# Two transformer blocks on one core: layer-norm factors from per-token sums, the later half's sums moved into the next stage, layers written out, the second block's first units in halves

## The reference, cut to what matters

```
y = _group_rmsnorm(mix, mix_g[l]) @ w_o[l]
x = _layernorm(ALPHA * x + y, ln1_g[l], ln1_b[l])
f = (jax.nn.silu(x @ w_gate[l]) * (x @ w_up[l])) @ w_down[l]
x = _layernorm(ALPHA * x + f, ln2_g[l], ln2_b[l])
...
h = x + 0.5 * swiglu(rms_norm(x, ffn1_norm[l]), ffn1_gate[l], ffn1_up[l], ffn1_down[l])
```

## Time and profile before

| | |
|---|---|
| median of 3 runs | 3297.21 us |
| the profiled execution's own time | 3301.32 us |
| its span, first to last instruction | 3299.5 us |
| TensorE matmuls busy | 3186.5 us, 97% of the span |
| VectorE, ScalarE, GpSimd busy | 1520.4, 714.4, 1967.7 us |
| granted TensorE clock, mean | 0.982 |

### The profile page before, as it was taken

One profiled execution on the slowest core, in us unless ns is written; L12 is line 12 of the kernel. 1 busy time (PEld: TensorE's weight loads), 2 busy tenths in 40 slices (PEclk: granted clock), 3 DMA queues, 4 the chain that ended last, 5 costly groups with the idle time before them and its releaser, 6 DMA issues.

```text
span 3299.5 us, 44938 instructions
## 1 busy us (share of the span) xinstructions
PE 3186.5 (97%) x15410; PEld 2620.2 (79%) x15410; DVE 1520.4 (46%) x1976; ACT 714.4 (22%) x1450; POOL 1967.7 (60%) x1566
## 2 busy tenths in 40 slices
PE   8998999989989999699999999999999999999998
PEld 7777888877778888588887778888888887778886
DVE  6577332275773231644327574432344237664422
ACT  3353110034532110411102231110111112321110
POOL 6334766653346666377766556776677666277763
PEclk9999999999999999899999999999999999999999
DMA  4111322221112222122223212222222232122231
GB/s 170 52 39 52 108 95 96 96 91 58 39 52 90 95 95 96 52 95 96 100 97 105 78 65 94 97 96 96 97 95 95 96 112 96 39 96 95 95 99 61
DMA packets 82023, 286.47 MB, mean 87 GB/s; under 512 B 9531, under 2 KB 13020, under 8 KB 81628
## 3 DMA queue, kind: packets, MB, share of 16 engines
q1 hardware_dynamic: 76032, 275.81, 24.8%
q10 hardware_dynamic: 5852, 8.78, 0.8%
HBM read 280.89 MB, written 3.67 MB: 86 GB/s over the span
## 4 chain that ended last, share of the span: by engine, by line
PE 91%; DVE 5%; issue 2%; ACT 1%; POOL 1%; DMA 0%; DVEq 0%; SPq 0%; ACTq 0%; POOLq 0%
PE bank_v L462 19%; PE bank_v L464 19%; PE bank_v L463 19%; PE bank_a L462 8%; PE bank_a L464 8%; PE bank_a L463 8%; PE bank_v L677 1%; PE bank_a L656 1%; PE bank_s L810 1%; PE bank_s L695 1%; PE bank_v L825 1%; PE bank_a L501 0%; DVE lru_x L1954 0%; PE bank_s L813 0%; PE bank_s L685 0%
## 5 line engine op out<-in xcount | busy, mean ns | idle before, releaser
L436 POOL TENSOR_TENSOR w_lo<-raw,w_hi 128x1024 fp32r<-128x1024 f32 x520 | 1319.4, 2537 | 41.7
L433 POOL TENSOR_TENSOR zero<-zero 128x1 f32<-128x1 f32 x520 | 128.0, 246 | 1253.8 <-PE bank_v L464 900.4
L462 PE MATMUL bank_v<-xn_hi,w_hi 128*128 128x512 f32 (+1 forms) x1680 | 645.5, 384 | 8.9 <-DVE resid L1505 4.5
L464 PE MATMUL bank_v<-xn_hi,w_lo 128*128 128x512 f32 (+1 forms) x1680 | 637.0, 379 | 0.0
L463 PE MATMUL bank_v<-xn_lo,w_hi 128*128 128x512 f32 (+1 forms) x1680 | 636.9, 379 | 0.0
L434 POOL CAST w_hi<-raw 128x1024 fp32r<-128x1024 f32 x520 | 555.0, 1067 | 0.0
L462 PE MATMUL bank_a<-xn_hi,w_hi 128*128 128x512 f32 (+1 forms) x1232 | 473.9, 385 | 40.3 <-DVE xn_lo L1477 21.5
L463 PE MATMUL bank_a<-xn_lo,w_hi 128*128 128x512 f32 (+1 forms) x1232 | 468.7, 380 | 0.0
L464 PE MATMUL bank_a<-xn_hi,w_lo 128*128 128x512 f32 (+1 forms) x1232 | 468.6, 380 | 0.0
L462 PE MATMUL bank_v<-h_hi,w_hi 128*128 128x512 f32 (+1 forms) x1100 | 419.7, 382 | 0.0
L464 PE MATMUL bank_v<-h_hi,w_lo 128*128 128x512 f32 (+1 forms) x1100 | 418.6, 381 | 0.0
(11 more groups left out here) (341 smaller groups left out, 3359.8 us busy)
## 6 DMA issues: line engine op xcount, KB each, us to landing
raw<-in_w_stream SPq DMA_DIRECT2D x520, 512.0 KB, 3.2
rope<-in_rope ACTq DMA_DIRECT2D x2, 1024.0 KB, 4.9
da_v<-t_rows ACTq DMA_DIRECT2D x2, 1024.0 KB, 5.7
out<-resid SPq DMA_DIRECT2D x4, 512.0 KB, 2.6
t_rows<-t_row ACTq DMA_DIRECT2D x1, 1536.0 KB, 5.7
resid<-in_x SPq DMA_DIRECT2D x4, 256.0 KB, 3.7
resid<-in_x ACTq DMA_DIRECT2D x4, 256.0 KB, 8.8
mla_v<-in_alibi ACTq DMA_DIRECT2D x2, 512.0 KB, 5.9
```

Of the source, the lines that this page charges most:

```text
L433: pool.tensor_tensor(zero[:, 1:2], zero[:, 0:1], zero[:, 0:1], ALU.add)
L436: pool.tensor_tensor(w_lo[:, u, :], raw[:, u, :], w_hi[:, u, :].bitcast(F32), ALU.subtract).then_inc(*w_split.done(("unit", u)))
L462: pe.matmul(out, lhs_hi, rhs_hi, start=first, stop=False)
L464: return pe.matmul(out, lhs_lo, rhs_hi, start=False, stop=last)
```

## The change

1. `ln_stats` makes sums per token instead of rows: the sums are now the stationary operand and one column of ones the moving one. Eight fp32 matmuls of 128 x 1 (two tiles, two sums, two sources) put mean and square sums of a half into four columns of `bank_s[0]`.
2. `factors(s)` works on tiles of 128 x 2. It then multiplies the identity by the reciprocal and by the offset, two 128 x 128 tiles each, and `ln_spread(tag, s)` on TensorE multiplies ones by these diagonals (two fp32 matmuls with 256 columns). `apply` reads both factors from two banks of PSUM instead of from `work` in SBUF.
3. `ln_stats(0)` moves to step 5 of the first, `ln_spread(0)` to step 5 of the second chunk of s=1 in `project_out`; in `down` they stand after steps 5 and 17 of the last chunk's s=1.
4. `ln_stats(1)` and `ln_spread(1)` of both norms stand in the next stage's `project_halves`, after its steps 1 and 8 of s=0. VectorE does factors(1) inside apply(0), after its step 5, ScalarE after its chunk 4. The lag is 3 instead of 4.
5. A root of one value stands at the head of each norm on ScalarE.
6. The last ln2 writes `xn_hi` and `xn_lo` with the second block's gain in its own passes; `gained("first")` goes. The first four units of the second block (gate0, up0, k=0,1) run in `project_halves` (`ffn_halves`). ScalarE makes the squares for `rms1` after apply(1), and then copies gate0's banks out; VectorE adds the squares, then copies up0's banks out; the sums for `rms1` and their spreading stand behind gate1,0 and up1,0.
7. The two layers of each block are written out instead of looped, with constants as semaphore targets (`laps`, `within`, `find` in `Counts` and `Signal`).

```diff
+LN_LAG = 3
...
+        def factor_banks(s):
+            return bank_s[1 + s], bank_s[0 if s else 3]
...
             def ln_stats(tag, s):
 
-                cut = HALVES[s]
-                b = bank_s[1 + s]
-                pe.wait_ge(*added.after(ln_key(tag, DC - 2, s, tag, "sum")))
-                pe.matmul(b[:, HALVES[0]], ones[:, :], ln_sum[:, cut], start=True, stop=False)
-                pe.wait_ge(*v_read.after(ln_key(tag, DC - 1, s)))
-                pe.matmul(b[:, HALVES[0]], ones[:, :], resid[:, DC - 1, cut], start=False, stop=True)
-                pe.wait_ge(*added.after(ln_key(tag, DC - 2, s, tag, "squares")))
-                pe.matmul(b[:, HALVES[1]], ones[:, :], ln_squares[:, cut], start=True, stop=False)
-                pe.wait_ge(*squared.after(ln_key(tag, DC - 1, s, tag)))
-                pe.matmul(b[:, HALVES[1]], ones[:, :], ln_square[:, (DC - 1) % 2, cut], start=False, stop=True
-                          ).then_inc(*sums.done((tag, "stats", s)))
+                pairs = (((ln_sum[:, :], added.after(ln_key(tag, DC - 2, s, tag, "sum"))),
+                          (resid[:, DC - 1, :], v_read.after(ln_key(tag, DC - 1, s)))),
+                         ((ln_squares[:, :], added.after(ln_key(tag, DC - 2, s, tag, "squares"))),
+                          (ln_square[:, (DC - 1) % 2, :], squared.after(ln_key(tag, DC - 1, s, tag)))))
+                for n, pair in enumerate(pairs):
+                    for _, ready in pair:
+                        pe.wait_ge(*ready)
+                    for t in range(2):
+                        column = bank_s[0][:, 4 * s + 2 * n + t:4 * s + 2 * n + t + 1]
+                        tile = slice((2 * s + t) * P, (2 * s + t + 1) * P)
+                        for k, (source, _) in enumerate(pair):
+                            mm = pe.matmul(column, source[:, tile], ones[:, 0:1], start=k == 0, stop=k == 1,
+                                           skip_group_check=True)
+                mm.then_inc(*sums.done((tag, "stats", s)))
+
+            def ln_spread(tag, s):
+
+                for n, name in enumerate(("rstd", "offset")):
+                    pe.wait_ge(*diag_ready.after((tag, name, s)))
+                    pe.matmul(factor_banks(s)[n][:, HALVES[1]], ones[:, :], work[:, 2 + s, HALVES[n]], start=True, stop=True,
+                              skip_group_check=True).then_inc(*sums.done((tag, name, s)))
...
+                            if s == 1 and k == 5:
+                                (ln_stats if c == DC - 2 else ln_spread)(tag, 0)
                             mm = mm3(b[:, cut], *w_tile(u, k), xn_hi[:, k, cut], xn_lo[:, k, cut], k == 0, k == DC - 1)
                         mm.then_inc(*(w_used.done(("wo", c)) if s else sums.done(("wo", c, s))))
-                        if s == 1 and c == DC - 2:
-                            ln_stats(tag, 0)
...
-                        if between and s == 0 and n == lag:
-                            between()
-
-            def down(tag, norm=None):
+                        if stats and s == 0 and n == 1:
+                            stats()
+                        if spread_factors and s == 0 and n == DC:
+                            spread_factors()
...
-                            if s == 1 and f == 8:
+                            if s == 1 and f == 5:
                                 ln_stats(norm, 0)
+                            if s == 1 and f == 17:
+                                ln_spread(norm, 0)
                     if norm and c == 2:
...
-                if norm:
-                    ln_stats(norm, 1)
...
+            def ffn_halves(tag):
+
+                project_halves([[((tag, "gate0", k), a_bank), ((tag, "up0", k), v_bank)] for k in range(2)],
+                               lambda c, s: x_lo.after(("ln2", c, s)), LN_LAG, *late_half("ln2", "layer1", DEPTH - 1))
+                project((tag, "gate1", 0), a_bank)
+                square_sums("rms1", added.after(("first", DC - 1)), ln_sum[:, :])
+                project((tag, "up1", 0), v_bank)
+                spread("rms1")
+                project((tag, "gate1", 1), a_bank)
+                project((tag, "up1", 1), v_bank)
+                ffn_rest(tag, 2)
+                down(tag, None, 2)
+
+            def late_half(tag, layer, l):
+
+                def stats():
+                    with counts.within(layer, l):
+                        ln_stats(tag, 1)
+
+                def spread_factors():
+                    with counts.within(layer, l):
+                        ln_spread(tag, 1)
+
+                return stats, spread_factors
...
-            with loop(pe, "layer1", DEPTH):
+            for l in counts.laps("layer1"):
                 project_halves(((("kr", v_bank), (("c", 0), a_bank)), ((("c", 1), a_bank), (("fk", 0), v_bank))),
-                               lambda c, s: x_lo.carried(("in1", c, s), ("ln2", c, s)), 4)
+                               lambda c, s: x_lo.carried(("in1", c, s), ("ln2", c, s)), LN_LAG,
+                               *(late_half("ln2", "layer1", l - 1) if l else ()))
                 project(("c", 2), a_bank)
...
-                               lambda c, s: x_lo.after(("ln1", c, s)), 4, lambda: ln_stats("ln1", 1))
+                               lambda c, s: x_lo.after(("ln1", c, s)), LN_LAG, *late_half("ln1", "layer1", l))
                 ffn_rest("ffn")
                 down("ffn", "ln2")
 
-            with loop(pe, "layer2", DEPTH):
-                ffn("ffn1", lambda c: x_lo.carried(("first", c), ("next", c)),
-                    ("rms1", added.carried(("first", DC - 1), ("next", DC - 1))))
+            for l in counts.laps("layer2"):
+                if l == 0:
+                    ffn_halves("ffn1")
+                else:
+                    ffn("ffn1", lambda c: x_lo.carried(("next", c), ("next", c)),
+                        ("rms1", added.carried(("next", DC - 1), ("next", DC - 1))))
                 project(("lg", 0), a_bank, is_split("rms2"))
...
                 def factors(s):
-                    mean, var = work[:, 2, HALVES[s]], work[:, 3, HALVES[s]]
-                    act.wait_ge(*dve_step.after((tag, "mean", s)))
-                    act.activation(var, mean, ACT.Square).then_inc(*act_step.done((tag, "mean2", s)))
                     act.wait_ge(*dve_step.after((tag, "var", s)))
-                    act.activation(var, var, ACT.Sqrt).then_inc(*rooted.done((tag, s)))
+                                   ).then_inc(*rooted.done((tag, s)))
...
+                act.activation(small[:, 30:31], ones[:, 0:1], ACT.Sqrt).then_inc(*act_step.done((tag, "root_table")))
...
+                apply(0, {1: lambda: square_of(DC - 1, 1), 4: lambda: factors(1)})
+                apply(1, {})
...
+                for k in range(2 * (done - 1)):
+                    leave_bank((tag, "gate0", k))
                 root(stats, 1)
...
                 def factors(s):
-                    cut, b = HALVES[s], bank_s[1 + s]
+                    mean, square, less, var, root, rstd, offset = (small[:, 16 * s + n:16 * s + n + 2]
+                                                                   for n in (0, 2, 4, 6, 8, 10, 12))
                     dve.wait_ge(*sums.after((tag, "stats", s)))
-                    step(dve.tensor_scalar(mean[:, cut], b[:, HALVES[0]], 1.0 / D, None, ALU.mult), (tag, "mean", s))
-                    step(dve.tensor_scalar(rstd[:, cut], b[:, HALVES[1]], 1.0 / D, 1e-5, ALU.mult, ALU.add),
-                         (tag, "square", s))
-                    dve.wait_ge(*act_step.after((tag, "mean2", s)))
-                    dve.tensor_tensor(var[:, cut], rstd[:, cut], var[:, cut], ALU.subtract).then_inc(*dve_step.done((tag, "var", s)))
+                    step(dve.tensor_scalar(mean, bank_s[0][:, 4 * s:4 * s + 2], 1.0 / D, None, ALU.mult), (tag, "mean", s))
+                    dve.tensor_scalar(square, bank_s[0][:, 4 * s + 2:4 * s + 4], 1.0 / D, 1e-5, ALU.mult, ALU.add
+                                      ).then_inc(*dve_step.done((tag, "square", s)))
+                    step(dve.scalar_tensor_tensor(out=less, in0=mean, scalar=-1.0, in1=mean, op0=ALU.mult, op1=ALU.mult),
+                         (tag, "less", s))
+                    dve.tensor_tensor(var, square, less, ALU.add).then_inc(*dve_step.done((tag, "var", s)))
                     dve.wait_ge(*rooted.after((tag, s)))
-                    step(dve.reciprocal(rstd[:, cut], var[:, cut]), (tag, "rstd", s))
-                    step(dve.scalar_tensor_tensor(out=offset[:, cut], in0=mean[:, cut], scalar=-1.0, in1=rstd[:, cut],
-                                                  op0=ALU.mult, op1=ALU.mult), (tag, "offset", s))
-
-                def apply(s, after_two=None):
-                    cut = HALVES[s]
+                    step(dve.reciprocal(rstd, root), (tag, "rstd", s))
+                    dve.scalar_tensor_tensor(out=offset, in0=mean, scalar=-1.0, in1=rstd, op0=ALU.mult, op1=ALU.mult
```

(33 more changed lines are left out.)

178 lines of the change are left out of this document (115 added, 63 removed).

## The result

The changed kernel takes 3309.98 us, the median of 7 runs (3307.74 to 3312.49), beside 3296.43 us of the kernel before on the same chip (7 runs, 3293.39 to 3306.37): a ratio of 1.0040, 95% interval 1.0029 to 1.0050. The whole interval lies above 1.002, so the change costs time. 3312 us had been forecast. The profiled execution took 3312.19 us, its span is 3310.4 us, and it shows 3209.0 us of busy TensorE (3186.5 before).

The account below looks back on a forecast made before the run. TensorE, busy for 97% of the span, was taken as the bound. Stages behind ln1 +16.8, layer 1's ln2 +5.9 and border -7.8 gave +14.9 us on 3297.2: 3312 us, range 3284 to 3324, its own 3305 to 3319.

Parts of the forecast that it names:

- stages of 34 to 38 us: Split stages behind the norms: a sign of the forecast, which put each at 36.5 us, 8.4 more than before behind ln1.
- waits of 2 to 3 us for the diagonals: TensorE at the spreading in each norm: waits for diagonals held by GpSimd, 2.5 us in ln1, 2.8 in ln2.
- wait of about 3 us inside the stages: Each split stage: TensorE wants xn_lo of chunk 3 at 4.1 us and gets it at 7.1, a 3.0 us wait.
- fifth unit: Split stages with lag 3: first pair's units free 2.2 us before the end, GpSimd needs 3.7; about 1.0 us wait.
- two and a half stretches like the one at 306.75: Low clock in each split stage: priced at 4.7 us lost, against 1.85 us before.
- row at 1976.04: Profile row: after a wait of only 1.35 us the window from 1976.80 shows clock 0.50; used to price short waits.
- one diagonal gets in between, the others are ready at 300.3: ln1: GpSimd casts from 296.2 and subtracts until 299.7, holding the diagonals; TensorE waits 2.5 us at the spreading.
- Rival B: GpSimd misses VectorE at the s=0 diagonals and first xn_lo, in all four norms: -15.3 us, 3282; chance 0.18.
- The border: Border of the two blocks: start 21.5 us earlier, units +8.7, later sums +1.7, gate0's bank +1.8, diagonals and hidden units +1.5: -7.8.
- The loop's turn: TensorE's 3.13 us standing at the first block's loop turn: counted as part of ln2's -4.0, the rest as nothing.
- rival D: The turn of the loop is cheap and its wait stays: +18.0 us, 3315; chance 0.03.
- Rival A: The clock stays as before, each of four stages losing 1.85 instead of 4.7 us: +3.5 us, 3301; chance 0.22.

Follow-up runs that it names:

- e8_sums_later: e3_late_factors with the later half's sums after TensorE's step 4 of the first half instead of step 1: 3293.67 us, ratio 0.9991.
- e3_late_factors: Changed kernel, but VectorE makes the later half's factors after step 8 instead of 5, ScalarE's root after chunk 7 instead of 4: 3299.24 us, ratio 1.0004.
- e10_adds_later: e8_sums_later with VectorE's two later-half additions in ln1 after its steps 4 and 5 instead of before steps 0 and 2: 3289.48 us, ratio 0.9982.
- e5_border: Kernel before with layers written out and only the border of the blocks changed; old norms, lag 4: 3280.16 us, ratio 0.9953.
- e4_unroll: Kernel before with its two blocks' layers written out and nothing else: 3295.89 us, ratio 0.9997.
- e11_layer2_only: Kernel before with only the second block's two layers written out; the first block stays a loop: 3295.92 us, ratio 0.9997.
- e7_late_fill: e3_late_factors with overwritten matmuls ahead of the first xn_lo (36) and of the later half (8): 3287.40 us, ratio 0.9978.
- e2_fill: Changed kernel with overwritten 256-column matmuls in TensorE's waits (36 before first xn_lo, 12 before fourth chunk, 8 before later half): 3297.93 us, ratio 1.0003.
- e6_border_fill: e5_border with overwritten 256-column matmuls, 56 ahead of the stage behind ln1, 38 ahead of ln2's later sums: 3281.20 us, ratio 0.9954.

## Why the prediction was right, and where its steps were not

The forecast of 3312 us and its sign held: +14.9 us in the sum, +13.6 by the medians, +10.9 between the two profiled executions. That it came so near is in part luck: several terms were off and partly cancelled. Of the signs that the forecast named, the stages of 34 to 38 us came (36.35, 36.47 and 36.57, the border's 39.04 with the bank's wait in it), and the low clock in them. The waits of 2 to 3 us for the diagonals did not, and the wait of about 3 us inside the stages was half as long.

**The split stages: the total right, its parts not.** 36.35 and 36.6 us stand against 36.5. But the 3.0 us wait for `xn_lo` of chunk 3 is 1.63, the spreading takes 0.67 instead of 0.9, and the clock costs 6.4 us instead of 4.7. Of the 1.0 us for the fifth unit, 0.63 shows behind ln1, where ScalarE's copy of a bank ends 0.1 us after GpSimd's subtraction (344.95 and 344.83), and 1.04 behind ln2. The failed step is "two and a half stretches like the one at 306.75". It took the low stretches from waits alone; e8_sums_later shows that with the same wait ahead of the stage the low stretch is 5.2 or 11.9 us, depending on where the sums stand. Even the row at 1976.04, from which the forecast took the price of a short wait, is one of one-column matmuls, so it did not tell the two apart. The two errors are linked: from the end of the sums (314.61) VectorE needs 3.2 us to `xn_lo` of chunk 3 where 3.7 were forecast, and TensorE, at half speed, 1.6 us for chunk 2 where 0.7 were forecast, so it comes later and waits less. That the factors in the middle of apply(0) are the costly wait was right: e3_late_factors gives 10.7 us back.

**GpSimd in the way: right in kind, wrong in what it caught.** The step "one diagonal gets in between, the others are ready at 300.3" failed: beside the cast four diagonals take 1.65 us, neither the 0.9 of an idle GpSimd nor a wait for its end, and they are ready 0.2 us after the subtraction's start in ln1 and at its start in ln2. So no wait stands at the spreading (2.5 to 2.8 us forecast), which makes ln2's start come 3.1 us sooner than forecast (-7.1 for -4.0) and the border's too (-24.6 for -21.5). At ln2 GpSimd did hold what the forecast said it would, the instructions ahead of the variance and the first `xn_lo`: 1.75 us instead of 0.15, and 2.27 instead of 0.41. In ln1 nearly nothing came of the early diagonals (-0.7 for 0), because the two additions, which the forecast did not list, stood behind GpSimd in their turn; e10_adds_later shows them to be worth 3 to 4 us over both layers. Rival B was worked out for diagonals and first `xn_lo` both free of GpSimd in all four norms; at ln2 only the diagonals were, at ln1 the additions took the place of the `xn_lo`, and its 3282 did not come.

**The border.** -7.8 was forecast; it is -24.6 + 17.1 = -7.5, each part some 3 us larger than forecast. The four units took 39.0 us for 36.5, 3.2 of it the wait for gate0's bank, priced at 1.8. e5_border shows what the sum hid: the border with the old norms wins 15 us.

**The loop's turn.** Priced at 3.1 us as part of the -4.0. In the trace of e4_unroll it is gone, as the row was read. So a compare-and-branch of about 108 ns, as the Trainium skill has it in "Advanced Engine Details and Errata", section "Control Flow Timing", is not the whole of what this turn takes, and rival D did not come. In the time nothing shows: the median of e4_unroll is 0.7 us under the kernel before's and equal to e11_layer2_only's, which has the turn. The term was right where it was read, but it does not reach the end.

**Not forecast at all.** +2.6 us before the first norm: partly the lag of 3, partly scatter of the start. The very first stage by halves ends at 46.2 to 49.1 us in the six traces with lag 3 and at 45.0 to 47.0 in the eight with lag 4. The wait for the second pair's unit in it (26.10, 2.43 us; 1.12 before) does not tell them apart: it is 1.1 to 2.7 us with lag 4 too. And -4.7 us around layer 2's attention, +1.7 in the second block. They nearly cancel. No run traces them to a cause; shifts of 3 us in that same attention also stand between e4_unroll and e11_layer2_only and between e5_border and e7_late_fill.

**The clock, by itself.** Rival A had it cost nothing more than before. e2_fill takes 12 us off by giving TensorE useless work in its waits, e7_late_fill 9 to 12 more off e3_late_factors. In e6_border_fill a like filling gives nothing: behind ln1 because VectorE sets the stage there, behind ln2 because the clock fell all the same. That the clock makes up a good part of the 29 us between the two forms of the norm is thus shown; why it stays low for longer with the one-column matmuls in front is not.

## What to carry to other kernels

Work that is moved into a stage is priced by what it stands in front of: the same factors cost about 11 us less three steps later on VectorE, and the same sums 4 to 6 us less three chunks later on TensorE. When a change bundles a gain and a loss, time the parts alone before judging the form: here one part won 15 us, the other lost 29 and, once its places, its lag and its clock were mended, nothing that could be measured (3280.5 against 3280.2). Filling a wait on TensorE with matmuls whose result is thrown away paid here where TensorE set the pace behind the wait, and gave nothing where VectorE did; read in a trace of the filled kernel whether the clock did stay up.

## What the runs showed of the hardware

- The granted clock stayed at 0.50 through 11.9 us of TensorE's unbroken work in e3_late_factors, with the eight one-column matmuls in it, and through 5.2 us in e8_sums_later, with them behind the rise (316.26 to 317.9); the wait ahead was 5.90 us in both.
- Four 128x128 `tensor_scalar` diagonals took 1.65 us while GpSimd was casting and 0.87 us while it was idle; `tensor_tensor` instructions on 128x256 with two SBUF operands took 2.15, 2.32 and 2.48 us instead of 0.41 where its subtraction was under way, and one with a PSUM operand 0.42 us beside the subtraction (e10_adds_later, 305.73).
- 38 matmuls of 256 columns ahead of each ln2's later sums and 56 ahead of each stage behind ln1 cost no time that could be measured (3281.20 against 3280.16).
